# Two fused transformer blocks on one core: stage borders by halves, rotary products on both row halves, and another spread of the gate's weights

## What is computed

```python
# first block
mod = silu(c) @ w_ada + b_ada;  shift, scale, gate = split(mod, 3)
h   = rms_norm(x) * (1 + scale) + shift
xr, gr, qc, kvc, kr, ga = split(h @ w_in)
y_rnn = rg_lru_branch(xr, ...) * silu(gr)      # width-4 convolution, two gates, linear recurrence over tokens
y_att = mla_branch(qc, kvc, kr, ...) * silu(ga) # 8 heads; a score is a 128-wide part plus a 64-wide rotary part
x   = x + gate * (concat([y_rnn, y_att]) @ w_out)
# second block
proj = rms_norm(x, norm_g) @ w_in_2            # q, k, v, gates, z_a, uv, z_b, merge logits
o_a = nsa_attention(...) * silu(z_a);  o_b = spatial_gating(...) * silu(z_b)
merged = g_a * (o_a @ w_up_a) + g_b * (o_b @ w_up_b)
x = x + merged @ w_out_2
x = x + sigmoid(x @ w_ple_gate) * (p @ w_ple)
out = rms_norm(x, final_g)
```

## Time and profile before

| | |
|---|---|
| median of 3 executions | 2532.26 us |
| the profiled execution | 2531.91 us |
| its span in the trace | 2530.2 us |
| TensorE busy | 2444.6 us (97% of the span) |
| ScalarE, VectorE, GpSimd busy | 826.3, 887.9, 1021.5 us |
| mean granted TensorE clock | 0.985 of full speed |

### The profile page before, as it was taken

The page is one execution under the profiler, slowest core; times in us unless marked ns, Lnnn a source line. Parts: engine busy times, 40 slices in busy tenths (PEclk is TensorE's granted clock), DMA queues, the critical chain, the costliest instruction groups (busy, mean ns, idle before and its releaser), DMA issues.

```text
span 2530.2 us, 28175 instructions
## 1 busy us (share of the span) xinstructions
PE 2444.6 (97%) x11092; PEld 1921.1 (76%) x11092; DVE 887.9 (35%) x1461; ACT 826.3 (33%) x1275; POOL 1021.5 (40%) x451
## 2 busy tenths in 40 slices
PE   7999999999999999999999999999999999999996
PEld 4666666667788888888787778787878787887885
DVE  4765356664210330040354534343421412202113
ACT  5234434433322422222343423343322312313222
POOL 1244322224565524444333333333334644445553
PEclk9899999999999999999999999999999999999998
DMA  7952133344344343333222233332333444453332
GB/s 298 396 223 77 53 118 121 102 137 135 100 147 142 114 158 100 92 100 94 73 76 75 72 100 96 92 105 84 105 94 98 145 147 129 125 162 117 92 100 83
DMA packets 97796, 308.50 MB, mean 122 GB/s; under 512 B 10497, under 2 KB 11905, under 8 KB 97537
## 3 DMA queue, kind: packets, MB, share of 16 engines
q1 hardware_dynamic: 97664, 306.71, 37.7%
HBM read 285.69 MB, written 20.97 MB: 121 GB/s over the span
## 4 chain that ended last, share of the span: by engine, by line
PE 84%; DVE 5%; DMA 3%; ACT 3%; issue 2%; SPq 1%; POOL 1%; DVEq 0%; ACTq 0%; POOLq 0%
PE bank L515 23%; PE bank L518 23%; PE bank L516 23%; DMA raw<-in_wst 2%; PE bank L511 2%; PE bank L512 2%; PE bank L514 2%; PE bank L994 2%; PE bank L1018 1%; PE bank L1006 1%; DVE gac L1708 1%; PE bank L934 1%; DVE S L1998 1%; DMA rawx<-in_wst 1%; POOL wlo L2453 1%
## 5 line engine op out<-in xcount | busy, mean ns | idle before, releaser
L2453 POOL TENSOR_TENSOR wlo<-raw,whi 128x1024 fp32r<-128x1024 f32 x356 | 871.7, 2453 | 1203.4 <-ACT whi L1109 1183.1
L515 PE MATMUL bank<-hhi,whi 128*128 128x512 f32 x2752 | 1093.0, 397 | 34.7 <-ACT whi L1109 19.3
L518 PE MATMUL bank<-hhi,wlo 128*128 128x512 f32 x2752 | 1081.4, 393 | 10.9 <-POOL wlo L2453 10.7
L516 PE MATMUL bank<-hlo,whi 128*128 128x512 f32 x2752 | 1078.4, 392 | 0.0
L515 PEld LDWEIGHTS bank<-hhi,whi 128*128 128x128 f32 x2752 | 520.1, 189 | 162.6 <-issue 32.7
L518 PEld LDWEIGHTS bank<-hhi,wlo 128*128 128x128 f32 x2752 | 519.9, 189 | 130.6 <-POOL wlo L2453 19.7
L516 PEld LDWEIGHTS bank<-hlo,whi 128*128 128x128 f32 x2752 | 520.4, 189 | 108.2 <-issue 1.7
L1109 ACT ACTIVATE whi<-raw 128x1024 fp32r<-128x1024 f32 x356 | 375.3, 1055 | 682.2 <-PE bank L518 479.7
L511 PE MATMUL bank<-whi,hhi 128*128 128x512 f32 x192 | 76.2, 397 | 4.4 <-DVE HID L2174 4.4
L2275 DVE TENSOR_SCALAR S<-S,sm 128x512 f32<-128x512 f32 (+1 forms) x64 | 78.0, 1219 | 0.6
L512 PE MATMUL bank<-whi,hlo 128*128 128x512 f32 x192 | 75.9, 395 | 0.0
(11 more groups left out here) (314 smaller groups left out, 2173.0 us busy)
## 6 DMA issues: line engine op xcount, KB each, us to landing
raw<-in_wst SPq DMA_DIRECT2D x407, 512.0 KB, 3.6
rawx<-in_wst SPq DMA_DIRECT2D x54, 512.0 KB, 6.5
rawy<-in_wst SPq DMA_DIRECT2D x24, 512.0 KB, 5.6
tgs<-TS SPq DMA_DIRECT2D x32, 256.0 KB, 3.8
axr<-tgs SPq DMA_DIRECT2D x32, 256.0 KB, 4.1
X<-in_xt SPq DMA_DIRECT2D x4, 1024.0 KB, 15.0
pls<-stg SPq DMA_DIRECT2D x16, 256.0 KB, 9.5
axr<-in_xt SPq DMA_DIRECT2D x16, 256.0 KB, 2.8
```

Source lines behind the costliest of these rows:

```text
L515: e.matmul(o, hi, xh, start=first, stop=False)
L516: e.matmul(o, hi, xl, start=False, stop=False)
L518: return e.matmul(o, lo, xh, start=False, stop=last)
L2453: e.tensor_tensor(sub(wlo, PAIR[c], CH), slots[slot(c)], sub(whi, PAIR[c], CH).bitcast(F), ALU.subtract).then_inc(*up("wlo_pool", "wlo", c))
```

## The change

Five parts. (1) At the four borders, HT tiles 0 to 7 are made while the last chunk of the old stage, which reads only tiles 8 to 15, still runs (at "o" the other way round: the last two chunks change places, and `upb` comes first). The next stage begins with the first chunks of its outputs 0 and 1 and then their second chunks (`led`), or, for the merge, with `upb` 0 and 1 before `upa` 0 and 1 in two more banks. VectorE makes all lower tiles; GpSimd none. (2) In a head's scores the two wide products of a pair of query blocks come first and the two rotary products follow, one on each half of the partitions; a copy of `QPE` with its halves exchanged (`QSW`) is made by eight DMAs of 128 KB. (3) A head takes four ticks. (4) The gate's 32 chunks are spread as 3+2 in rounds 0 to 3, 2+2 in rounds 4 to 6 and none in round 7. (5) `KCT` and `VCC` are cleared some chunks earlier.

```diff
+GATED = [3, 2, 3, 2, 3, 2, 3, 2, 2, 2, 2, 2, 2, 2, 0, 0]
+MERGE = [(n, br, ("upa", "upb")[br]) for n, br in [(0, 1), (1, 1), (0, 0), (1, 0)]
+         + [(n, br) for n in range(2, 15) for br in (1, 0)] + [(15, 0), (15, 1)]]
...
+    def led(name):
+        out.extend((name, n, h) for h in range(2) for n in range(2))
+        blocks(name, range(2, 16), 2)
...
     for c in range(8):
-        blocks("win1", [c], 2)
-        out.extend(gate[4 * c:4 * c + 2])
-        blocks("win1", [8 + c], 2)
-        out.extend(gate[4 * c + 2:4 * c + 4])
+        for half in range(2):
+            blocks("win1", [8 * half + c], 2)
+            out.extend(gate[at:at + GATED[2 * c + half]])
+            at += GATED[2 * c + half]
...
-    blocks("w2f", range(32, 40), 2)
-    for n in range(16):
-        out.append(("upa", n, 0))
-        out.append(("upb", n, 0))
-    blocks("wout2", range(16), 2)
-    blocks("pleg", range(16), 2)
+    blocks("w2f", range(32, 39), 2)
+    out.extend([("w2f", 39, 1), ("w2f", 39, 0)])
+    out.extend((name, n, 0) for n, br, name in MERGE)
+    led("wout2")
+    led("pleg")
...
+            def led(name, st):
+                to = [claim(ring("main"), "proj", name, n) for n in range(2)]
                 for h in range(2):
+                    for n, (o, prior) in enumerate(to):
+                        feature_block((name, n, h), HT[8 * h:8 * h + 8], [(st, k) for k in range(8 * h, 8 * h + 8)],
+                                      h == 0, h == 1, o[:, :], prior, (name, n))
...
-            def unit_scores(u, score):
+            def unit_scores(u, nope, rope):
                 bks = [claim(ring("side"), "score", u, n) for n in range(3)]
-                for i in (3, 2, 0, 1):
...
+                for two in ((3, 2), (1, 0)):
+                    for i in two:
+                        n, off = places(i)
+                        for f in bks[n][1]:
+                            w.wait_ge(*f)
+                        nope(i, bks[n][0][:, off:off + P * (i + 1)])
+                    for i in two:
+                        n, off = places(i)
+                        rope(i, bks[n][0][:, off:off + P * (i + 1)]).then_inc(*up("score_pe", "score", u, i))
...
+                    def rope(i, o):
                         cols, wd = slice(P * i, P * (i + 1)), P * (i + 1)
+                        if i % 2:
+                            return e.matmul(o, qp[:, cols], KR[pb:pb + 64, 0:wd], start=False, stop=True)
+                        return e.matmul(o, QSW[ps:ps + 64, cols], KR[ps:ps + 64, 0:wd], start=False, stop=True)
...
+                    w.wait_ge("qsw", 32 * (h // 2 + 1))
+                    unit_scores(("a1", h), nope, rope)
                     yield
                     yield
                     unit_transposes(("a1", h), S1)
+                    yield
                     yield
...
-            for n in range(16):
+            led("wout1", "y")
+            for n in range(2, 16):
                 project("wout1", n, "y")
-                tick()
...
+            for i, (n, br, name) in enumerate(MERGE):
+                o, prior = claim(ring("side" if i in (2, 3) else "main"), "proj", name, n)
```

ScalarE at border "y" ("o", "m" and "x2" are alike):

```diff
             for h in range(8):
                 use()
                 tick()
                 use()
+                if h == 7:
+                    for k in range(8):
+                        upper(k, sub(YR, k), "y", [done("y", k), done("used", INDEX["win1", 32, 0])])
                 w.wait_ge(*done("proj", "win1", 25 + h))
...
-            for k in range(16):
-                upper(k, sub(YR, k) if k < 8 else sub(QN, k - 8), "y", [done("y", k), done("proj", "win1", 32)])
+            for k in range(8, 16):
+                upper(k, sub(QN, k - 8), "y", [done("y", k), done("proj", "win1", 32)])
```

VectorE at "y" and at "m":

```diff
+                if h == 7:
+                    for k in range(8):
+                        lower(k, sub(YR, k), "y", [done("y", k), done("used", INDEX["win1", 32, 0])])
                 w.wait_ge(*done("ga", h))
...
-            for k in range(0, 16, 2):
-                lower(k, sub(YR, k) if k < 8 else sub(QN, k - 8), "y", [done("y", k), done("proj", "win1", 32)])
+            for k in range(8, 16):
+                lower(k, sub(QN, k - 8), "y", [done("y", k), done("proj", "win1", 32)])
...
+            def merged_lower(k):
                 w.wait_ge(*done("hhi", "m", k))
                 w.wait_ge(*done("mg", k))
-                w.wait_ge(*done("proj", "upb", 15))
+                w.wait_ge(*done("proj", ("upa", "upb")[k // 8], 15))
...
+                if i == 31:
+                    for k in range(8):
+                        merged_lower(k)
```

GpSimd:

```diff
-            for k in range(1, 16, 2):
-                lower(k, sub(YR, k) if k < 8 else sub(QN, k - 8), "y", [done("y", k), done("proj", "win1", 32)])
             for n in range(16):
-                use(2)
+                use({0: 3, 1: 1}.get(n, 2))
...
             w.wait_ge(*done("rsb"))
+            e.memset(KCT[:, :], 0.0).then_inc(*up("fill_pool"))
+            e.memset(VCC[0:64, :], 0.0).then_inc(*up("fill_pool", "blank"))
             for kv, pe_ in enumerate(("pe_k", "pe_v")):
...
             use(INDEX["w2sv", 0, 0] - turn["use"])
-            e.memset(KCT[:, :], 0.0).then_inc(*up("fill_pool"))
-            e.memset(VCC[0:64, :], 0.0).then_inc(*up("fill_pool", "blank"))
```

SyncE:

```diff
+            def swapped(a):
+                for p in (0, 64):
+                    e.dma_start(QSW[p:p + 64, :], QPE[64 - p:128 - p, a * NT:(a + 1) * NT]).then_inc(*up("qsw", by=16))
             for c in range(8):
+                if c in (2, 4, 6):
+                    for i in range(4):
+                        w.wait_ge(*done("score", ("a1", c - 1), i))
+                    swapped(c // 2)
                 load(INDEX["win1", c, 0] + (7 if c else 3))
+                if c == 0:
+                    for key in HEADKEYS:
+                        w.wait_ge(*done("head", *key))
+                    swapped(0)
                 w.wait_ge(*done("xpad"))
```

More of the change, by code:

```diff
@@ L860, in tensor @@
                 tick()
-                next(gate_it)
-                next(gate_it)
+                for _ in range(GATED[2 * c]):
+                    next(gate_it)
                 project("win1", 8 + c, "h")
                 tick()
[L865 to L868, removed]
+                for _ in range(GATED[2 * c + 1]):
+                    next(gate_it)
             for h in range(8):
@@ L2089, in vector @@
                 sg["c"] = c
-                next(gate_it)
-                next(gate_it)
-            while heads["n"] < 8:
-                tick()
+                for _ in range(GATED[2 * c + 1]):
+                    next(gate_it)
             for h in range(8):
@@ L2380, in vector @@
                 y, s = sub(Q2, i), SU[i % 2][:, :]
+                if i == 7:
+                    for k in range(8, 16):
+                        lower(k, sub(OB, k - 8), "o", [done("ob", k - 8), done("used", INDEX["w2f", 39, 1])])
                 w.wait_ge(*done("za", i))
@@ L2413, in vector @@
                     *up("lo_dve", "hlo", "m", k))
+            begun = set()
+            for i, (n, br, name) in enumerate(MERGE):
+                if i == 31:
+                    for k in range(8):
+                        merged_lower(k)
+                second = n in begun
+                begun.add(n)
+                w.wait_ge(*done("proj", name, n))
+                w.wait_ge(f"ax{i % 8}", 32 + 16 * (i // 8 + 1))
+                for k in range(16):
+                    w.wait_ge(*done("hhi", "o", k))
+                    w.wait_ge(*done("hlo", "o", k))
+                if n >= 2:
+                    w.wait_ge(*done("mg", n - 2))
+                second_done(w)
+                e.scalar_tensor_tensor(m2t[n % 2][:, :] if second else sub(MG, n), AXR[i % 8][:, :], 1.0,
+                                       bank("proj", name, n)[:, :], ALU.add, ALU.mult).then_inc(
+                    *up("mg_dve", "mgp", i, frees=("proj", name, n)))
+                if second:
+                    w.wait_ge(*now("mg_dve"))
+                    e.tensor_tensor(sub(MG, n), sub(MG, n), m2t[n % 2][:, :], ALU.add).then_inc(*up("mg_dve", "mg", n))
@@ L2414, in vector @@
+            for k in range(8, 16):
+                merged_lower(k)
             for n in range(16):
+                if n == 15:
+                    for k in range(8):
+                        lower(k, sub(X2, k), "x2", [done("res", "wout2", k), done("used", INDEX["wout2", 15, 0])])
                 w.wait_ge(*done("proj", "wout2", n))
```

122 lines of the change are left out of this document (44 added, 78 removed).

## The result

The changed kernel takes 2503.91 us (median of four runs, 2500.04 to 2508.3); the kernel before, run beside it, 2529.79 (2526.47 to 2532.32). The ratio is 0.9899 with a 95% interval of 0.9883 to 0.9914: 1% faster, where 2484 us (1.9%) was forecast, and 2 us above the range. The profiled run took 2500.82 us with a span of 2499.1, so it gained 31.1 us on the profiled run of before; 47.7 were forecast.

A forecast was written before the change was run, and what follows sets the result against it. TensorE, busy 97% of the span, was taken as the bound. Gains of 23.0 (borders), 6.2 (fillings), 12.7 (rotary) and 5.8 (rounds) sum to 47.7; 2531.9 less that gives 2484 us, range 2470 to 2502.

The forecast's parts named there:

- Borders: Four stage borders: stops and the slow clock behind them go, 25.0 us lost, 0.5 left at each; gain 23.0 us.
- the third chunk's lower half: At each border: GpSimd's lower weight half, held behind VectorE's lower tiles, ready 0.7 us late; 0.5 us taken per border.
- keep ahead: At the borders: VectorE makes lower tiles in 0.61 us each, while one is due each 0.68 us.
- Fillings: At the compression: clearing `KCT` and `VCC` earlier leaves about 1.2 us of 7.4 lost; gain 6.2 us.
- Rotary products: In each head's scores: two halves overlap and fewer changes of height, 5.78 to 4.19 us; gain 12.7 for eight heads.
- Rounds: Eight rounds: four steps per head and the new gate spread leave 12 of 18 lost us; gain 5.8, bounds 2 and 30.
- a PEclk below 0.95 in the rounds: Sign of being wrong: TensorE's mean clock in the eight rounds falls below 0.95.
- 7.2 us from gate chunk to usable weights: In the rounds: from VectorE's gate chunk through load and both halves 7.2 us, making next round's first chunk 1.5 late.
- the convolution ends just as the recurrence products start: In rounds 0 to 3: timing assumed for the late-weights chain, the half ready 10.2 us behind the recurrence products' start.
- The starvation of round 7: Round 7: its gate chunks make weights late, 7.9 us lost; without gate chunks there these go.
- the 4.5 of the waits on PT: In the rounds: values two chunks behind their transposes remove the waits on PT, 4.5 us plus restarts.
- the rounds stay starved: Rival: later loads in the rounds cost 18 to 30 us, gain there 0 to -12, total 2490 to 2502; chance 0.17.

The follow-up runs named there:

- e6: Kernel before with borders and fillings alone (three steps per head, even gate spread, old order of scores): 2496.9 us, ratio 0.9876.
- e7: e1 with all rotary products of a head on its own half of the partitions, new order of scores kept: 2476.5 us, ratio 0.9795.
- e5: e1 with the scores in the order of the kernel before, the exchanged copy made but not used: 2479.9 us, ratio 0.9808.
- e1: Changed kernel with gate chunks spread evenly, two in each of sixteen places, four steps per head kept: 2473.5 us, ratio 0.9776.
- e4: Changed kernel with three steps per head and the even gate spread: 2498.9 us, ratio 0.9875.
- e12_gates: e1 with VectorE's second pair of gate chunks in each round ahead of the recurrence's last step (scan): 2467.5 us, ratio 0.9758.
- e2: Changed kernel with gate spread 3,2,3,2,3,3,2,2 then twos, so the second gate sum stands one place later: 2493.0 us, ratio 0.9855.
- e8: Changed kernel with the head's exponentials ahead of the weight split on ScalarE in each round: 2496.2 us, ratio 0.9870.
- e3: Kernel before with four steps per head, one step added ahead of the values, nothing else: 2509.6 us, ratio 0.9919.
- e11: Kernel before with an empty fourth step per head behind the values: 2514.1 us, ratio 0.9940.
- e10_convxp: e1 with probabilities scaled behind the convolution, and the convolution's input copied ahead of a weight split: 2478.9 us, ratio 0.9801.

## Why the prediction was wrong, point by point

**Borders: right in size; what is left has another cause.** 23.0 us were forecast with 0.5 left at each, 23.1 came, with 0.30 to 0.76 left; e6 gives 31.6 for borders and fillings together (29.7 without the opening), where 29.2 were forecast. The prediction put the rest on the third chunk's lower half, held on GpSimd behind VectorE's lower tiles. No such wait is there. TensorE waits once at each border, for one of VectorE's lower tiles, which were to "keep ahead" at 0.61 us each: at "y" eight take 11.50 us beside two subtractions on GpSimd, and a single one up to 2.88. That the 0.5 fits is luck. The Trainium skill (GPSIMD Engine Reference, section Key points) names contention between GpSimd and VectorE instructions with two SBUF inputs; the trace agrees, but the engine that TensorE waits for is VectorE.

**Fillings: right.** 6.2 forecast, 6.7 came; the wait left, 0.5 us, is for a small step of VectorE (`HID`, L2203), where 1.2 us were estimated to stay.

**Rotary products: right on TensorE, wrong in time.** 12.7 forecast and 13.2 measured as TensorE's time; the same prices, put together for one half in the expectation of e7, give 5.05 us, and 4.99 were measured. But the term entered the sum in full, and 6.4 (e5 to e1) or nothing (e6 to e4) passes on: where other engines follow TensorE closely, less work on TensorE turns into waits. This was not weighed. With the gate chunks of e12_gates there are no waits: 235.1 us from the first scores to the recurrence's products of round 7, 13.3 less than e5_turns, so there the whole 13.2 seems to pass on (e12 with the scores as before was not run).

**Rounds: the step that failed.** "So 12 of 18 us remain, in other places; bounds 2 and 30. Gain 5.8." From the first scores to the recurrence's products of round 7 the changed kernel takes 265.6 us (316.4 to 582.0) and e5_turns, which has no stop there, 248.4 with 13.2 us more of scores: 30.4 us are lost, and some 2 more behind that point at half clock, 32 in all and above even the upper bound; with 14.6 lost where 5.8 were to be won, this one term makes the miss of 16.6 us (20.4, less 1.1 that the other parts gave over their forecast and the 2.7 of the opening). One of the prediction's signs of being wrong came with it: a PEclk below 0.95 in the rounds, 0.82 in round 3. The term held three errors.

- *The gate sum was left out.* The chunks' move was costed by their VectorE time and their loads alone. TensorE's sums move with them, and one of them landed in the same place as the chunk that it needs: 10.9 us (e2).
- *The late load was followed on one engine only.* The chain "7.2 us from gate chunk to usable weights" was right as far as it went: the waits on `wlo` are there and short. But the split that waits for the load stands on ScalarE ahead of the exponentials, and behind these come softmax and convolution on VectorE: with "the convolution ends just as the recurrence products start" the prediction set that wait at nothing, and it is 9.0 us, with restarts at half clock. The 5.8 us of rounds 1 and 2 go with the order on ScalarE (e8); 3.6 us of waits on the convolution stay with the even spread (e1).
- *The starvation of round 7 was put down to its gate chunks.* It went with four steps per head, with the gate chunks still there (e3, e11). So the fourth step was worth 17 to 19 us (e6 to e5, before to e3), not the 4.5 of the waits on PT, and the new spread, made for round 7, bought nothing and cost 26 to 30.

The rival "the rounds stay starved" (0.17), with its reason that the loads hang on VectorE's order and get more gate work in rounds 0 to 3, is the case that came nearest, a little beyond its upper end of 2502; its reason covers the late loads, not the gate sum, which none of the rivals names. Part by part the change reads, in medians: 31.6 for borders and fillings, 17.1 for four steps, 6.4 for the rotary part, and 30.4 lost to the spread: 24.7, beside 25.9 measured between the medians of the pair. Each part is the difference of two neighbours in one chain of kernels, so that the sum fits is no evidence; and the parts hang on their order, as the rotary part shows, which is worth nothing ahead of the four steps.

## What to carry to other kernels

When a step is moved, list what it does on *every* engine and mark the in-order queue it is moved in: here a four-product sum on TensorE cost more than the move could have gained. Follow a late load past the engine that waits for it, to all that stands behind that wait in the queue, and on to the engines these feed. Work that is spread evenly over the rounds feeds the loads evenly: look for rounds that lack a piece of work before blaming the loads in them, and check a cut in the busy engine's work for what its neighbours can follow.

## What the runs showed of the hardware

A GpSimd instruction held VectorE up even where VectorE's instruction is tiny. In e1_even (timelines of VectorE and GpSimd) a step on 128x4 numbers took 1.74 us, and ended within 0.03 us of GpSimd's subtraction (416.40 + 2.43 = 418.83); in e12_gates, with GpSimd idle, the same step took 0.17. In seven of the eight rounds of e1_even this step met a subtraction; it took 1.15 to 2.21 us there and ended within 0.03 us of it each time, while the subtraction kept its 2.4.

```profile
417.12 1.74 DVE L2018 TENSOR_SCALAR sm<-sm 128x4 f32<-128x4 f32 x1
...
416.40 2.43 POOL L2496 TENSOR_TENSOR wlo<-rawy,whi 128x1024 fp32r<-128x1024 f32 x1 [7.95 <-ACT whi L1138]
```

The scaling of the probabilities, with one tensor operand too, took 3.4 to 3.5 us beside GpSimd and 1.28 alone (e10_convxp). The Trainium skill (SBUF — State Buffer, section SBUF: two separate sides) says that, of a GpSimd instruction and a VectorE instruction in a two-port mode or with two SBUF inputs, the one that starts first holds the shared ports for its whole length and the other is blocked. The matching ends agree with that, and they show that steps with one tensor operand are held too; whether these run in such a mode no run here shows.
